# Scan of a two-block network on one core: the spread of cumulative sums and its causal mask taken from TensorE to DMA and GpSimd

## What is computed

```python
def step(state, inp):
    xq, aq, bq, cq = inp
    a_cum = jnp.cumsum(aq, axis=1)
    seg = a_cum[:, :, None] - a_cum[:, None, :]
    decay = jnp.exp(jnp.where(tril, seg, -jnp.inf))
    scores = jnp.einsum('btgn,bsgn->btsg', cq, bq)
    y_diag = jnp.einsum('btsg,btsgr,bsgrp->btgrp', scores, decay, xq)
    ...
```

## Time and profile before

| what | value |
|---|---|
| median of 3 runs | 912.71 us (912.67 to 915.16) |
| the profiled execution | 913.4 us, of which 911.5 are the span of the trace |
| TensorE busy | 893.2 us (98% of the span) |
| VectorE, ScalarE, GpSimd busy | 658.8, 540.0, 311.0 us |
| HBM | 200.3 MB read, 221 GB/s over the span |
| the scan beside the steps | from 134 to 256 us |

### The profile page before, as it was taken

How to read it: one execution, slowest core, us unless ns; L and a number is a source line. 1 busy time by engine, 2 the same in 40 slices (tenths; PEclk the granted TensorE clock), 3 DMA queues, 4 the chain that set the end, 5 groups by cost and what they waited for, 6 DMA issues and landing times.

```text
span 911.5 us, 17859 instructions
## 1 busy us (share of the span) xinstructions
PE 893.2 (98%) x7386; PEld 859.8 (94%) x7386; DVE 658.8 (72%) x879; ACT 540.0 (59%) x848; POOL 311.0 (34%) x269
## 2 busy tenths in 40 slices
PE   9999999999999999999999999989999999999998
PEld 7899999999999999999999999978888999999998
DVE  5878977887687777868888767678985487754442
ACT  5378555557967873486665444557786765444431
POOL 2153324444387621276654111220003652122100
PEclk9999999999999999999999999999999999999999
DMA  8764555666676678843988887423433448755560
GB/s 349 319 239 177 186 228 184 243 235 247 229 300 243 244 256 313 288 163 141 340 301 298 299 304 278 164 93 139 140 116 116 146 176 324 277 188 174 181 224 24
DMA packets 36258, 202.50 MB, mean 222 GB/s; under 512 B 4945, under 2 KB 6225, under 8 KB 17490
## 3 DMA queue, kind: packets, MB, share of 16 engines
q1 hardware_dynamic: 36178, 201.37, 61.3%
HBM read 200.30 MB, written 1.05 MB: 221 GB/s over the span
## 4 chain that ended last, share of the span: by engine, by line
PE 74%; issue 13%; POOL 5%; ACT 4%; DVE 4%; POOLq 0%; ACTq 0%; DVEq 0%
PE acc L1218 60%; PE m L1218 3%; ACT w_hi L768 2%; POOL rt L656 1%; PE acc L1181 1%; PE m L1181 1%; POOL ul L662 1%; PE m L1157 1%; PE m L1294 1%; PE m L1152 1%; DVE fr L1500 1%; POOL maps L712 1%; PE m L1411 1%; POOL ycl L662 0%; PE m L1356 0%
## 5 line engine op out<-in xcount | busy, mean ns | idle before, releaser
L1476 DVE TENSOR_TENSOR w_lo<-raw,w_hi 128x2048 fp32r<-128x2048 f32 (+1 forms) x140 | 307.7, 2198 | 134.6 <-ACT w_hi L768 134.4
L1218 PE MATMUL acc<-uh,w_hi 128*128 128x256 f32 x1224 | 346.0, 283 | 2.7 <-POOL ul L662 2.1
L1218 PE MATMUL acc<-ul,w_hi 128*128 128x256 f32 x1224 | 339.9, 278 | 0.0
L1218 PE MATMUL acc<-uh,w_lo 128*128 128x256 f32 x1224 | 339.8, 278 | 0.0
L768 ACT ACTIVATE w_hi<-raw 128x2048 fp32r<-128x2048 f32 x140 | 264.3, 1888 | 76.6 <-PE acc L1218 76.3
L1218 PEld LDWEIGHTS acc<-uh,w_hi 128*128 128x128 f32 x1224 | 230.8, 189 | 9.1 <-issue 4.2
L1218 PEld LDWEIGHTS acc<-ul,w_hi 128*128 128x128 f32 x1224 | 230.8, 189 | 0.4 <-issue 0.2
L1218 PEld LDWEIGHTS acc<-uh,w_lo 128*128 128x128 f32 x1224 | 230.4, 188 | 0.0
L1218 PE MATMUL acc<-hidh,w_hi 128*128 128x256 f32 x432 | 119.2, 276 | 0.0
L1218 PE MATMUL acc<-hidl,w_hi 128*128 128x256 f32 x432 | 119.2, 276 | 0.0
L1218 PE MATMUL acc<-hidh,w_lo 128*128 128x256 f32 x432 | 119.2, 276 | 0.0
(11 more groups left out here) (383 smaller groups left out, 1723.6 us busy)
## 6 DMA issues: line engine op xcount, KB each, us to landing
raw<-in_tiles SPq DMA_DIRECT2D x136, 1024.0 KB, 5.7
colw<-in_ada_cols SPq DMA_DIRECT2D x80, 512.0 KB, 5.7
ada_w<-in_ada_tiles SPq DMA_DIRECT2D x8, 1024.0 KB, 18.2
raw<-in_rest SPq DMA_DIRECT2D x4, 768.0 KB, 4.8
xT<-in_x SPq DMA_DIRECT2D x2, 512.0 KB, 7.3
first_w<-in_tiles SPq DMA_DIRECT2D x1, 1024.0 KB, 11.6
colw<-in_tiles SPq DMA_DIRECT2D x1, 1024.0 KB, 17.5
out<-xT SPq DMA_DIRECT2D x8, 128.0 KB, 3.9
```

Of the source, the lines that this page charges most:

```text
L1218: ins = pe.matmul(o, l, r, start=(s.k == 0 and i == 0 and not j), stop=(s.last and i == s.kts - 1 and j == 2))
L1476: dve.tensor_tensor(lo, raw_, hi.bitcast(F32), ALU.subtract).then_inc(S("lo_ready"), 1)
```

## The change

The cumulative sums of a head are no longer spread by TensorE. At CUM_AT ScalarE copies them (32 heads, unsplit) to `cum_r` and its queue writes them to a tensor in HBM, `cum_rows`; from the next step on its queue reads each head's row back, repeated over the 128 partitions, into one of seven row buffers (five in `mc`, two in `seg`; four of them from head 21 on, since "co" writes `mc`). The first seven are loaded ahead, row p later at the slot behind the last use of its buffer: six slots ahead of its own for p < 21, three from there on. GpSimd masks a row (`causal`, an affine select) one slot ahead of its exponential, ScalarE reads the row from SBUF. On GpSimd the low parts of a "cb" step are done a step later, behind that step's head products. M1 and M2 are free of the spread; the transposes move there, three slots later (XT_SLOT 24), and the late conv outputs to M3 and M4. VectorE no longer splits the sums, and has two waits at "co" for exponentials.

```diff
 CONV_BANKS = ["acc0", "acc1", "acc2", "M0", "M1", "M2", "M3", "M4", "acc0", "acc1", "acc2", "M1", "M2", "M3", "M4", "acc0"] +\
-    (4 * ["acc1", "acc2", "M1", "M2", "acc0"])[0:16]
+    (4 * ["acc1", "acc2", "M3", "M4", "acc0"])[0:16]
...
-    XT_SLOT = 21
+    XT_SLOT = 24
...
+    def row_slot(q):
+        return q % 7 if q < 21 else 3 + (q - 21) % 4
+    def row_before(q):
+        return None if q < 7 else q - 7 if q < 21 else q - 4
+    row_use = [sum(row_slot(p) == row_slot(q) for p in range(q + 1)) for q in range(HEADS)]
+    cum_rows = nc.dram_tensor("cum_rows", (HEADS, 3 * P), F32).ap()
...
+            def causal(q):
+                ends = row_of(q).rearrange("p (a b) -> p a b", b=P)[:, 0:3:2, :]
+                pool.wait_ge(S(f"row_in{row_slot(q)}"), 16 * row_use[q])
+                pool.affine_select(out=ends, in_=ends, compare_op=ALU.is_ge, fill=NEG, base=0,
+                                   pattern=[[0, 2], [1, P]], channel_multiplier=-1).then_inc(S("causal"), 1)
...
-                    if s.kind == "cb":
-                        lo_part(YC + NB * s.j + nb)
                     q = NB * (n - SCAN0) + nb
+                    if -1 <= q < HEADS - 1:
+                        causal(q + 1)
                     if 0 <= q < HEADS:
                         pool.wait_ge(S("exp_done"), q + 1)
                         pool.wait_ge(S("sc_done"), q // 4 + 1)
                         pool.tensor_tensor(EXS[q % 4], EXS[q % 4], sc[:, q // 4 % 2, :], ALU.mult).then_inc(S("mul_done"), 1)
+                if n and steps[n - 1].kind == "cb":
+                    for nb in range(NB):
+                        lo_part(YC + NB * steps[n - 1].j + nb)
...
+            def load_row(q):
+                act.dma_start(row_of(q), cum_rows[q:q + 1, :].to_broadcast([P, 3 * P])).then_inc(S(f"row_in{row_slot(q)}"), 16)
...
-                        act.wait_ge(S("bc_done"), q + 1)
+                        act.wait_ge(S("causal"), q + 1)
                         if q >= 4:
                             act.wait_ge(S("y_done"), q - 3)
-                        bank = (M1, M2)[q % 2]
-                        act.activation(EXS[q % 4][:, 0:T], bank[:, 0:T], ACT.Exp, bias=nac[:, 0, q:q + 1])
+                        if q:
+                            for p in range(HEADS):
+                                if row_before(p) == q - 1:
+                                    act.wait_ge(S("exp_done"), q)
+                                    load_row(p)
+                        row = row_of(q)
+                        act.activation(EXS[q % 4][:, 0:T], row[:, 0:T], ACT.Exp, bias=nac[:, 0, q:q + 1])
...
-                        act.activation(cum_t[0:2 * HEADS, 0:T], M0[0:2 * HEADS, T:2 * T], ACT.Copy).then_inc(S("cum_hi"), 1)
+                        act.activation(cum_r[0:HEADS, :], M0[0:HEADS, T:2 * T], ACT.Copy).then_inc(S("cum_row"), 1)
+                        act.wait_ge(S("cum_row"), 1)
+                        act.dma_start(cum_rows[:, 0:T], cum_r[0:HEADS, :]).then_inc(S("cum_out"), 16)
+                        act.dma_start(cum_rows[:, T:3 * P], cum_r[0:HEADS, P:T]).then_inc(S("cum_out2"), 16)
...
-                    pe.matmul(bank[:, 0:3 * P], pick[:, q:q + 1].to_broadcast([P, P]), cum_t[:, :], start=True,
-                              stop=False)
-                    pe.matmul(bank[:, 0:3 * P].rearrange("p (a b) -> p a b", b=P)[:, 0:3:2, :], ident_r[:, :],
-                              mask_r[:, :].unsqueeze(1).to_broadcast([P, 2, P]), start=False, stop=True)\
-                      .then_inc(S("bc_done"), 1)
...
-                bank = ("M3", "M4")[i % 2]
+                bank = ("M1", "M2")[i % 2]
...
-                        low = cum_t[HEADS:2 * HEADS, 0:T]
-                        link(dve.tensor_tensor(low, M0[HEADS:2 * HEADS, T:2 * T], low.bitcast(F32), ALU.subtract))
-                        dve.tensor_copy(cum_t[0:2 * HEADS, T:3 * P], cum_t[0:2 * HEADS, P:T].bitcast(F32)).then_inc(S("cum_done"), 1)
```

More of the change, by code:

```diff
@@ L451, in wait_raw, with row_of @@
             eng.wait_ge(S(raw_name(n)), 16 * ((n - 2) // NRAW + 1) if n >= 2 else 16)
+        mcf = mc[:, :, :].rearrange("p a b -> p (a b)")
+        def row_of(q):
+            k = row_slot(q)
+            return mcf[:, k * 3 * P:(k + 1) * 3 * P] if k < 5 else seg[:, k - 5, :]
         N_FIRST = 7
-        N_CONST = 29
+        N_CONST = 28
         def drained(s, nb):
@@ L1049, in _ @@
                             act.wait_ge(S("nac_done"), 1)
-                        act.wait_ge(S("bc_done"), q + 1)
+                        act.wait_ge(S("causal"), q + 1)
                         if q >= 4:
                             act.wait_ge(S("y_done"), q - 3)
-                        bank = (M1, M2)[q % 2]
-                        act.activation(EXS[q % 4][:, 0:T], bank[:, 0:T], ACT.Exp, bias=nac[:, 0, q:q + 1])
-                        act.activation(EXS[q % 4][:, T:T + P], bank[:, T:T + P], ACT.Exp, bias=nac[:, 1, q:q + 1])\
+                        if q:
[5 more added lines that the diff above has]
+                        act.activation(EXS[q % 4][:, 0:T], row[:, 0:T], ACT.Exp, bias=nac[:, 0, q:q + 1])
+                        act.activation(EXS[q % 4][:, T:T + P], row[:, T:T + P], ACT.Exp, bias=nac[:, 1, q:q + 1])\
                            .then_inc(S("exp_done"), 1)
@@ L1078, in _ @@
                         act.wait_ge(S("ac_done"), 1)
-                        act.activation(cum_t[0:2 * HEADS, 0:T], M0[0:2 * HEADS, T:2 * T], ACT.Copy).then_inc(S("cum_hi"), 1)
+                        act.activation(cum_r[0:HEADS, :], M0[0:HEADS, T:2 * T], ACT.Copy).then_inc(S("cum_row"), 1)
+                        act.wait_ge(S("cum_row"), 1)
+                        act.dma_start(cum_rows[:, 0:T], cum_r[0:HEADS, :]).then_inc(S("cum_out"), 16)
+                        act.dma_start(cum_rows[:, T:3 * P], cum_r[0:HEADS, P:T]).then_inc(S("cum_out2"), 16)
+                    at = NB * (n - CUM_AT - 1) + nb
+                    if 0 <= at < 4:
+                        if at == 0:
+                            act.wait_ge(S("cum_out"), 16)
+                            act.wait_ge(S("cum_out2"), 16)
+                        for q in range(2 * at, min(2 * at + 2, 7)):
+                            load_row(q)
                 if n == SOFT_AT:
@@ L1290, in scan_slot @@
                     pe.wait_ge(S("mul_done"), h + 1)
+                    pe.wait_ge(S("xdt_done"), h // 2 + 1)
                     take("M4")
@@ L1394, in _ @@
                             pe.matmul(o, tri[:, 0:P], dta[:, t, 0:HEADS], start=(t == 0), stop=True)
-                        pe.matmul(M0[0:2 * HEADS, T:2 * T], dta[:, 0, :], tri[:, :], start=True, stop=False)
-                        pe.matmul(M0[0:2 * HEADS, T + P:2 * T], dta[:, 1, :], tri[:, 0:P], start=False, stop=True)\
+                        pe.matmul(M0[0:HEADS, T:2 * T], dta[:, 0, 0:HEADS], tri[:, :], start=True, stop=False)
+                        pe.matmul(M0[0:HEADS, T + P:2 * T], dta[:, 1, 0:HEADS], tri[:, 0:P], start=False, stop=True)\
                           .then_inc(S("ac_done"), 1)
-                        free["M0"] = ("cum_done", 1)
+                        free["M0"] = ("nac_done", 1)
                     zs = n - Z0
@@ L1738, in _ @@
                         dve.wait_ge(S("gate"), NB * s.j + nb + 1)
+                        if s.j == 0:
+                            dve.wait_ge(S("exp_done"), 20)
+                        elif s.j == 2:
+                            dve.wait_ge(S("exp_done"), HEADS)
                         dve.tensor_tensor(mc[:, NB * s.j + nb, :], ps, gt[:, nb, :], ALU.mult).then_inc(S("gate_used"), 1)
```

18 lines of the change are left out of this document (5 added, 13 removed).

## The result

| kernel | median | span and execution of the profiled run |
|---|---|---|
| before, on the same chip | 912.91 us (12 runs) | 911.5 and 913.4 us |
| changed | 915.59 us (913.52 to 917.54, 12 runs) | 913.5 and 915.27 us |

The account below looks back on a forecast made before the run. TensorE, busy 98%, was taken to bound the kernel. Gain -11.3, stall +5.9, clock +1.5 and pace +1.0 summed to -2.9 us, from the median 912.7 to 909.8 us; range 905.3 to 913.5.

Parts of the forecast that it names:

- spread and mask matmuls: Two TensorE matmuls for each of 32 heads go, saving 0.29 or 0.38 us a slot, 10.0 us in all.
- the transposes' wait: TensorE's 0.81 us wait before the third token transpose goes, VectorE having caught up three slots later: 0.8 us saved.
- waits for a product: Two TensorE waits of 0.24 us for a head's product, behind a low part on GpSimd, go: 0.5 us saved.
- stall at "co": TensorE waits at the 7th and 8th k-tile of "co" for late "cb" low parts: 5.9 us, from 4.5 to 8.5.
- the clock behind it: TensorE's clock falls to half in the stall and part of the stretch behind: 1.5 us lost, bounds 0 and 1.7.
- the pace of the runs: Runs of 24 products turn slower, 0.10 us each: taken +1.0 us, between -1.0 and +2.4.
- What it removes: On TensorE, the spread and mask matmuls, the transposes' wait and two waits for a product go: 11.3 us gained.
- E itself comes 0.96 earlier against VectorE ...: 0.8: E, the start of the last "cb" product on TensorE, advances against VectorE, busy from 198.43: 0.8 us more stall.
- VectorE's pace: Rival: in the scan VectorE, needing 17.9 of 20.3 us per three steps, limits TensorE; half of 10.0 lost, 915; chance 0.05.
- The rule quoted with the prediction: GpSimd and two-SBUF-input VectorE instructions share a port pair under exclusive lock; a mask may wait out a 2.2 us subtraction.
- What is hidden: Masks on GpSimd (13 us), row loads, the HBM write and VectorE's new waits cost nothing unless a rival holds.
- The rival on the other side: Head products come late at pair slots, TensorE waiting 1.2 us each; at 5 of 16 slots +6, 916 us; chance 0.07.

Follow-up runs that it names:

- the filler run: The changed kernel with 32 matmuls on constants put ahead of the 7th k-tile of the first "co": 913.27 us, ratio 0.9997 to the kernel before.
- two ahead: The changed kernel with low parts behind the product, masks of rows 0 to 20 done two slots ahead instead of one: 910.52 us, ratio 0.9964 to before.

## Why the prediction was wrong, step by step

The account of the changed kernel's trace, worked out from the starts of products, beside the terms of the prediction:

| term | predicted | in the trace |
|---|---|---|
| spread and mask matmuls | -10.0 | -10.1 (gaps 1.30 to 1.01, 0.40 to 0.12, 1.07 to 0.69) |
| the transposes' wait | -0.8 | -0.2 (1.0 less at 99.30, 0.8 more at 100.77) |
| waits for a product | -0.5 | -0.6 |
| stall at "co" | +5.9 | +6.9 |
| the clock behind it | +1.5 | +2.2 (2.6 by the filler run) |
| the pace of the runs | +1.0 | +1.4 (1.7 in the scan, -0.3 ahead of it) |
| new waits for VectorE up to slot 22 | 0 | +1.7 |
| start, and all behind the scan | 0 | +0.6 |
| sum | -2.9 | +1.9 |

The two spans differ by 2.0 us. No single term makes the miss of 4.8: 1.7 are the new waits for VectorE, which the prediction put at nothing, 1.0 the stall, 0.7 the clock, 0.6 the transposes, 0.4 the pace, and 0.6 are the start, which is not the change's; two terms came out 0.2 better.

**What it removes: right in the matmuls, wrong in the wait.** 0.29 and 0.38 a slot came out to the hundredth. The wait of 0.81 ahead of the transposes is gone, but TensorE, now earlier, stands 0.66 for a low part of weights in the next run, which takes 3.54 us instead of 2.70. The kernel before with only its transposes moved shows the same (0.68 at 99.73), so the prediction's "it has caught up with that: 0.8" failed by itself:

```profile
100.77 0.38 PE L1265 MATMUL m<-uh,w_hi 128*128 128x256 f32 x1 [0.66 <-POOL w_lo L722]
```

The stretch of 0.9 in the table of starts above is three transposes that moved into the scan and a faster pace; little of it is a wait saved.

**The stall: the mechanism was right, its size too small, and the step that failed is "E itself comes 0.96 earlier against VectorE ...: 0.8".** I advanced TensorE against VectorE only from 198.43 on, where VectorE last had a pause. The groups over the scan show what that leaves out. Before, VectorE waited for the pair's matmuls at every addition to `xs`; these waits were its slack, and they are spent after the change:

```profile
L1584 DVE SCALAR_TENSOR_TENSOR xs<-xs,dsk,m 128x256 f32<-128x256 f32 x10 | 4.8, 480 | 10.1 <-PE m L1297 10.1
L1476 DVE TENSOR_TENSOR w_lo<-raw,w_hi 128x2048 fp32r<-128x2048 f32 x12 | 28.2, 2352 | 3.7 <-ACT w_hi L768 3.7
```

```profile
L1621 DVE SCALAR_TENSOR_TENSOR xs<-xs,dsk,m 128x256 f32<-128x256 f32 x11 | 5.2, 471 | 0.4 <-PE m L1334 0.4
L1513 DVE TENSOR_TENSOR w_lo<-raw,w_hi 128x2048 fp32r<-128x2048 f32 x12 | 32.5, 2704 | 6.2 <-ACT w_hi L800 6.2
```

(134 to 220 us, before and changed; the last column is the idle time ahead of the group.) TensorE's last product of "cb" came 4.93 us earlier (211.81 to 206.88), VectorE's product from which ScalarE's chain starts only 0.84 (212.22 to 211.38). So E advanced by 4.1 us against VectorE, where the prediction had 0.8, and 0.3 for masks. The second low part was ready at E + 18.7, not E + 15.8 (the first, for which the stall waits, at E + 18.0). TensorE reached the 7th k-tile at E + 11.1, which is E + 11.4 for the 8th, not E + 9.9, since it had itself waited for VectorE in slots 21 and 22. Part of the error doesn't need TensorE's advance: in the kernel before with late low parts, where the same sum gave 3.4, the wait is 4.37. The errors in the low parts and in TensorE's arrival both come from VectorE and partly cancel. That the stall came within 1.0 us of the forecast is luck to that extent.

**VectorE's pace, given 0.05, held in part.** The 915 of that rival lies close to the 915.6 measured, but not by its sum: TensorE's waits for VectorE are 1.7 us, not 5, and most of the loss is the stall and the clock. What is right in it is that VectorE's slack was used up. I took busy time (17.9 of 20.3 us in three steps) for the measure. That left 2.4 us, but busy time isn't fixed. For the same 23 slots VectorE is busy 69.5 us before and 74.7 after, and idle 16.0 and 6.4: 4.4 of the 9.6 went into TensorE's advance, 5.2 into its own longer work. The runs show that the masks don't explain this: it is 75.1 without rows and masks, with low parts behind the product, and 74.4 in the kernel before with nothing changed but the place of its low parts. Three more products of transposed tokens fall into the stretch (96 instructions instead of 93), and the rest is mostly longer instructions, the subtractions of weights above all (28.2 to 32.5 us for the same 12). I think that they take longer by the GpSimd instruction that each meets, which differs with every shift of the order. The rule quoted with the prediction (the Trainium skill, "SBUF — State Buffer", "SBUF: two separate sides", the exclusive lock) agrees with rows such as these of the changed kernel:

```profile
186.16 1.69 POOL L737 TENSOR_TENSOR exb<-exb,maps 128x384 f32<-128x384 f32 x1 [0.51 <-ACT exb L1092]
187.81 2.46 POOL L714 TENSOR_SCALAR_AFFINE_SELECT mc<-mc 128x256 f32<-128x256 f32 x1
...
186.90 3.10 DVE L1513 TENSOR_TENSOR w_lo<-raw,w_hi 128x2048 fp32r<-128x2048 f32 x1
```

The subtraction, 2.29 us elsewhere, starts beside a product and takes 3.10; the mask, 0.40 elsewhere, ends 0.27 us behind it. No run removes the lock by itself.

**What is hidden: masks were not.** "Free, unless a rival below holds" cost 3.4 to 3.9 us where the order lets it be measured. 32 masks are 13 us in my count; in the trace they take 30.5. The loads were close to free (0.2 to 0.7 us, not told from nothing), though two rows came late: GpSimd stood 0.90 and 4.13 us for them at 210.22 and 235.75, and no wait of TensorE stands behind either.

**The clock and the pace** were right in kind. I took one low stretch, 3.4 us, for the fall; the low level lasted from 222.0 to 228.8, 3.9 us of it behind the stall. In the pace I misread the kernel before. Not 10 of its 34 runs are slow: 24 take 2.70 to 2.74, nine take 2.61 or 2.62, and one, the last, 2.81. With all at 2.71 only 0.9 could be lost. In the changed kernel three take 2.61 and twelve take 2.8, a third pace: 1.1 of the 1.7 lost in the scan are its work. That the +1.0 was near is luck.

**The rival on the other side**, products late at the slots of pairs, did not occur in the changed kernel, but it is what the orders with low parts ahead of the product ran into, once a "cb" step: the place of the low parts, which I read only as a cost, is what kept it away.

What is not settled: what sets the pace of 0.1133, 0.1178 or 0.122 us, by which path the masks cost their 3.4 to 3.9 us (two ahead, the waits only changed place), how much of VectorE's longer busy time is the lock, and whether the changed kernel's own loss of 2.4 us would go with its new waits for VectorE: no run takes these alone.

## What to carry to other kernels

Before adding up what a fast engine saves, look for the idle time of the engine beside it that ends with the fast one (here 10.1 us at one line): that is all the saving that this neighbour can follow, and its busy time may grow with every shift against a third engine. In a queue that runs strictly in order, put what others wait for ahead of what waits for others: with its low parts ahead of the mask the changed kernel is 9.7 us slower than before, ahead of the product 0.7 slower, behind it 3.0 faster. And price the parts of a change apart: here 64 matmuls less were worth 7.1 us at best (low parts behind the product, no rows and no masks), masks took back half, and the place of one instruction more than what was left.

## What was not expected of the hardware

In the scan TensorE's clock fell in or behind each wait of over 3 us (6.94, 4.37, 4.25, 3.77, 3.30, 3.14). Of the shorter ones it fell behind 1.73, 1.95, 2.08, 2.22, 2.40 and 2.63, and not behind 1.76, 1.84, 1.85, 2.03, 2.06, 2.19, 2.23 and 2.70. The wait of 2.44 to 2.50 us in the attention stands in all 18 traces, and the clock fell at it in 11 of them: the length of a wait alone doesn't decide. It stayed up through 7.07 us of matmuls on constants. GpSimd's affine select on 128x256 took from 0.40 to 2.46 us in the changed kernel. The same 24 products took 2.61 or 2.71 us, and 2.73 or 2.81 behind a pair, with no wait in between, and which of them depends on which matmuls stand ahead.
